# A one-core decoder step: TensorE's 32 experts written out, its next token count read in mid-block, one looped body on ScalarE and VectorE, the second biases in mid-way, the last keys' load one place earlier

## The chip, the cores and the metric

One core of one Trainium2 chip runs the whole program, all in 32-bit floats. The metric is the device time of one execution in microseconds (us), and the number to be compared is the median of the runs.

## The reference, cut to what matters

288 tokens (256 of a prompt, 8 x 4 new ones) go through one layer: a combined projection, dilated attention beside a state-space mixer, an output projection, and then a mixture of 32 experts of which each token takes four.

```python
logits = jnp.dot(h, w_router) + b_router
top_v, top_i = lax.top_k(logits, TOP_K)                    # 4 of 32
gates = jax.nn.softmax(top_v, axis=-1)
...
def expert_block(args):                                    # w1[e]: 1024 x 2048, w2[e]: 1024 x 1024
    a = jnp.dot(xb, w1[e]) + b1[e]
    x_glu = jnp.minimum(a[:, :D_FF], SWIGLU_LIMIT)
    x_lin = jnp.clip(a[:, D_FF:], -SWIGLU_LIMIT, SWIGLU_LIMIT)
    mid = x_glu * jax.nn.sigmoid(SWIGLU_ALPHA * x_glu) * (x_lin + 1.0)
    return jnp.dot(mid, w2[e]) + b2[e]
...
out = out.at[row_tok].add(ys * row_gate[:, None])          # back to the tokens, by gate
```

Every expert's weights are read whole: 12 MB each, 384 MB in all. Before that, eight batches of cached keys and eight of cached values are read (1.25 MB each).

## The kernel before, in words

**The front** is hand-ordered. SyncE (`sp`) issues all transfers of data in one queue, in program order. `load_keys(b)` brings the keys of batch b into one of two buffers and, from batch 2 on, first waits until TensorE has turned the 5 key tiles of each batch up to b-2 (`kt_ps`). `load_values(b)` brings values into one of four buffers. The last batches are issued in the order values 4, values 5, keys 7, values 6, values 7 (L435 to L439). TensorE turns the key tiles in `key_columns(n)` (L1414; batch 7 is n = 35 to 39), takes the scores in L1431 and L1433, and applies the values in `values(half)` (L1457). VectorE and ScalarE evict the key tiles in turn (L1016, L690).

**The expert stage.** The weights of an expert are 12 pieces of 1 MB, in the places of a ring of 21 slots, which lie in nine different tiles (`ring`, `kv_rows`, `tmp`, `w_glu`, `mixer`, `uni`, `accT`, `x`, `low`). So a slot's name repeats after 7 experts (`TURNS`), since 7 x 12 = 4 x 21. SyncE refills a slot (L491) as soon as TensorE has used its piece for the last time (`w_used`, and `out_ps` for the twelfth piece).

An expert's tokens are served in blocks of 32, so an expert with up to 32 tokens takes one block, one with up to 64 two, and so on; the weights are loaded once for all of them. `run_experts` finds the blocks of an expert with three nested loops over the count (L339 to L344), read from `cnt` (L337). In this input there are 51 blocks. The experts 0 and 1 come first, for their weights can be loaded before the routing is known; the others come in an order that spreads the full ones.

A block on TensorE (`pe_pass`): the first product, 8 pieces, four matmuls in quadrants each (L1739); adding the block before back to the tokens (L1716); gathering the tokens of the next block (L1684), for which it waits for `sel`, made by VectorE (L1248); transposes (L1764, L1769); the second product, 4 pieces (L1747); transposes of the gathered tokens (L1727) and the first bias of the next block (L1732). ScalarE's part is a sigmoid and two copies (L801 to L805). VectorE's (`next_block`) is the selection of the next block, the gating, four evictions, and eight small products for the gated selection (L1217, L1218). VectorE is thus one block ahead of TensorE in its loops, and reads two registers from memory for each expert (count and name), TensorE and ScalarE one.

On each of the three engines the expert loop is written as a loop of four passes over a body of 7 experts (L350), and four more experts behind it. TensorE adds the second biases for all tokens (`second_biases`, L1700) between the two, behind the 28th expert. SyncE has a loop of its own (L498), which is not changed.

Of the kernel before, what the change touches and what calls it, by code (L numbers as in the profile page):

```python
# [35 lines left out]
NTOK = SEQ + NS  # L36
# [21 lines left out]
NPIECE = 12  # L58
NSLOT = 21
TURNS = 7  # L60
WARM = 20


# [58 lines left out]
def decoder_step(nc, I, O):  # L122

    with ExitStack() as ctx:
# [189 lines left out]
        def landed(turn, k):  # L314
            return s_w[(NPIECE * turn + k) % NSLOT]
# [12 lines left out]
        def expert_at(eng, place):  # L328
            return eng.value_load(names_o[0:1, bass.ds(place, 1)], min_val=0, max_val=NEXP - 1)

        def run_experts(eng, block_of, named=False, between=None):

            done = eng.alloc_register()
            eng.reg_mov(done, 0)

            def expert(turn, e, before):
                count = eng.value_load(cnt[0:1, bass.ds(e, 1)], min_val=1, max_val=NTOK)  # L337
                name = expert_at(eng, e) if named else None
                with eng.Fori(0, 2 * CAP, CAP) as p:  # L339
                    with eng.If(count > p):  # L340
                        with eng.Fori(p, 2 * p + CAP, CAP) as o:
                            with eng.If(count > 2 * o - p):
                                with eng.Fori(2 * o - p, 6 * o - 4 * p + CAP, CAP) as c:
                                    with eng.If(count > c):  # L344
                                        n = eng.snap(done, min_val=0, max_val=NEXP * CHUNKS)
                                        first = nc.s_assert_within(c, 0, CHUNKS * CAP - CAP, skip_runtime_bounds_check_because="p, o, c of the three loops give 0; 1, 2; 3 to 8 times CAP")
                                        block_of(n, turn, name, before, first)
                                        eng.reg_add(done, done, 1)

            with nc.Fori(0, NEXP // TURNS, engines=[eng.engine], hint_back_edge=eng is nc.tensor) as g:  # L350
                for turn in range(TURNS):
                    expert(turn, g * TURNS + turn, g * (16 * TURNS * NPIECE // NSLOT))
            if between:
                between()
            for turn in range(NEXP % TURNS):
                expert(turn, NEXP // TURNS * TURNS + turn, 16 * (NEXP // TURNS * TURNS * NPIECE // NSLOT))
            return eng.snap(done, min_val=NEXP, max_val=NEXP * CHUNKS)


# [1 line left out]
        def _(sp):  # L361
# [56 lines left out]
            def load_values(b):  # L418
                load_cache("cache_v", v_cache[:, b % 4, :], b, S[f"vload{b % 4}"])
# [13 lines left out]
            sp.dma_start(w_out, I["w_out"][0].rearrange("(j p) n -> p j n", p=P)).then_inc(S["wout"], 16)  # L433
            sp.wait_ge(S["pv"], 1)
            load_values(4)  # L435
            load_values(5)
            load_keys(7)
            load_values(6)
            load_values(7)  # L439

# [178 lines left out]
        def _(act):  # L619
# [176 lines left out]
            act.wait_ge(S["gT_ps"], 1)  # L796
            A(gT[0:2 * NEXP, :], ps[0:2 * NEXP, 7, SEQ:SEQ + P], ACT.Copy)
            A(gT[2 * NEXP:, 0:NS], ps[2 * NEXP:3 * NEXP, 7, SEQ:SEQ + NS], ACT.Copy).then_inc(S["gT"], 1)
            def act_pass(n, turn, e, before, first):
                act.wait_ge(S["glin"], n + 1)  # L800
                A(sig, glu_b, ACT.Sigmoid, scale=ALPHA).then_inc(S["sgm"], 1)  # L801
                act.wait_ge(S["selT_ps"], n + 1)
                A(selT, ps[:, 5, 0:3 * P], ACT.Copy).then_inc(S["selT"], 1)  # L803
                act.wait_ge(S["out_ps"], n + 1)
                A(y, ps[:, 7, 0:NQ], ACT.Copy).then_inc(S["y"], 1)  # L805
# [16 lines left out]
        def _(dve):  # L822
# [432 lines left out]
                dve.wait_ge(S["sel"], n + 1)  # L1255
                gated_selection(bc(gate[:, bass.ds(e, 1), :].rearrange("p e t -> p (e t)").unsqueeze(2), [P, 3, CAP]))

            def dve_pass(n, turn, e, before, first):

                with dve.If(n > 0):  # L1260
                    next_block(n, e, first)
# [22 lines left out]
        def _(pe):  # L1284
# [446 lines left out]
                for q in range(4):  # L1731
                    mm(hidden(q), pick[quarter(q), :], b1_rows[quarter(q), :].rearrange("p (g n) -> p g n", g=2), start=True, stop=False, skip_group_check=True)  # L1732

            def pe_pass(n, turn, e, before, first):

                def first_product(k):
                    pe.wait_ge(landed(turn, k), before + loads(turn, k))
                    for q in range(4):
                        ins = mm(hidden(q), xe[:, k % 2, quarter(k // 2)], slot(turn, k)[:, :, NQ * q:NQ * q + NQ], start=False, stop=(k == 7),  # L1739
                                 skip_group_check=True)  # L1740
                    return ins

                def second_product(k):
                    pe.wait_ge(landed(turn, k), before + loads(turn, k))
                    for m in range(2):
                        for q in range(4):
                            ins = mm(ps[quarter(q), 7, 0:NQ], mt[:, m, quarter(k - 8)], slot(turn, k)[:, m, NQ * q:NQ * q + NQ],  # L1747
                                     start=(k == 8 and m == 0), stop=(k == 11 and m == 1), skip_group_check=True)
                    return ins

                pe.wait_ge(S["xe"], n + 1)
                for k in range(8):
                    ins = first_product(k)
                    if k == 7:
                        ins.then_inc(S["hid"], 1)
                    else:
                        ins.then_inc(S["w_used"], 1)
                pe.wait_ge(S["y"], n + 1)
                sum_back(0)
                sum_back(1).then_inc(S["w_used"], 1)  # L1760
# [62 lines left out]
```

## Time and profile before

| | |
|---|---|
| median of 3 runs | 1233.45 us (1232.19 to 1235.42) |
| the profiled execution | 1228.69 us, of which the profile's span is 1226.9 us |
| TensorE matmuls busy | 1087.5 us, 89% |
| VectorE, ScalarE busy | 412.0 us (34%), 218.4 us (18%) |
| queue of all data transfers | 445.00 MB, 89.8% of the 16 DMA engines' span |
| TensorE's mean granted clock | 0.949 |

The expert stage runs from 252 us to 1214 us of the span. The shares are means over the span; a stage can be bound by something that has a lower share in the whole. The profile says "issue" where an engine waited for nothing that it shows, which takes in the time of the engine's own register, branch and load-register instructions.

### The profile page before, as it was taken

What the parts mean: (1) busy time and instruction counts of PE and PEld (TensorE: products, weight loads), DVE (VectorE), ACT (ScalarE), POOL (GpSimd) and SP (SyncE); (2) the same over time, 40 slices, a digit from 0 to 9 for tenths busy, and PEclk for the clock granted to TensorE, in tenths of its full rate; (3) what the DMA queues carried; (4) which work ended last, traced back from release to release, by engine and by line L of the source; (5) the groups of instructions that cost most, each with busy time, mean ns of one, the idle gap of its engine ahead of it and who ended that gap; (6) DMA issues with size and microseconds to landing.
All of it is one profiled execution on the core that took longest, in us unless ns stands there. A gap on an engine that the chain in (4) does not pass through costs nothing.

```text
span 1226.9 us, 29914 instructions
## 1 busy us (share of the span) xinstructions
PE 1087.5 (89%) x10891; PEld 500.8 (41%) x10892; DVE 412.0 (34%) x1237; ACT 218.4 (18%) x402; POOL 81.8 (7%) x117
## 2 busy tenths in 40 slices
PE   8997889999988798999998786899989968999985
PEld 7775455444433333344433232244334422444442
DVE  4999665442212222222222221122222211222221
ACT  3214432311101011111111010011111100110111
POOL 2179300000000000000000000000000000000000
PEclk8998999999989998999999798799989998998999
DMA  8617775946999999998999999999999999999996
GB/s 231 231 44 237 267 272 218 357 193 272 419 420 419 421 413 419 420 417 333 419 421 419 419 419 419 421 384 420 419 418 376 418 420 421 412 419 419 419 420 248
DMA packets 81042, 446.46 MB, mean 364 GB/s; under 512 B 16801, under 2 KB 18145, under 8 KB 32033
## 3 DMA queue, kind: packets, MB, share of 16 engines
q1 hardware_dynamic: 80928, 445.00, 89.8%
q8 instruction: 65, 1.06, 0.4%
q14 instruction: 49, 0.39, 0.1%
HBM read 442.46 MB, written 2.51 MB: 363 GB/s over the span
## 4 chain that ended last, share of the span: by engine, by line
PE 62%; DMA 13%; SPq 12%; issue 7%; DVE 3%; ACT 1%; DVEq 1%; POOL 0%; POOLq 0%
PE ps L1739 21%; PE ps L1747 11%; SPq L491 10%; DMA ring<-in_w_moe_dram 6%; PE ps L1684 4%; PE ps L1332 4%; PE ps L1716 3%; PE ps L1732 3%; PE ps L1604 2%; DMA low<-in_w_moe_dram 2%; DMA uni<-in_w_moe_dram 2%; DMA kv_rows<-in_w_moe_dram 2%; PE ps L1714 1%; PE ps L1727 1%; PE ps L1764 1%
## 5 line engine op out<-in xcount | busy, mean ns | idle before, releaser
L1739 PE MATMUL ps<-ring,uni 128*32 128x512 f32 x2008 | 250.7, 638 | 50.8 <-issue 35.1
L1739 PEld LDWEIGHTS ps<-ring,uni 128*32 128x32 f32 x2008 | 64.4, 115 | 229.7 <-issue 193.4
L1233 DVE TENSOR_SCALAR uni<-ps 128x256 f32<-128x256 f32 x51 | 21.6, 424 | 298.2 <-PE ps L1739 298.2
L1747 PE MATMUL ps<-ring,uni 128*32 128x256 f32 x1696 | 100.3, 381 | 7.4 <-DMA ring<-in_w_moe_dram 7.4
L801 ACT ACTIVATE uni<-uni 128x256 f32<-128x256 f32 x51 | 21.2, 416 | 427.0 <-DVE uni L1233 427.0
L1254 DVE COPY uni<-ps 128x256 f32<-128x256 f32 x50 | 21.2, 425 | 211.2 <-PE ps L1727 211.2
L1684 PE MATMUL ps<-uni 128*32 128x256 f32 x1248 | 80.1, 390 | 8.3 <-DVE uni L1248 8.0
L801 ACT ACT_TABLE_LOAD x51 | 65.4, 1283 | 85.1 <-issue 85.1
L1747 PEld LDWEIGHTS ps<-ring,uni 128*32 128x32 f32 x1696 | 51.9, 110 | 46.5 <-DMA ring<-in_w_moe_dram 11.8
L1332 PE MATMUL ps<-accT,ring 128*128 128x288 f32 x256 | 66.4, 418 | 0.3 <-issue 0.3
L1716 PE MATMUL ps<-uni 32*128 32x256 f32 x832 | 62.1, 414 | 0.0
L1248 DVE TENSOR_TENSOR uni<-low,uni 128x96 f32 x50 | 12.9, 259 | 143.5 <-issue 133.6
L1716 PEld LDWEIGHTS ps<-uni 32*128 32x128 f32 x832 | 39.1, 192 | 47.5 <-issue 46.0
L1332 PEld LDWEIGHTS ps<-accT,ring 128*128 128x128 f32 x256 | 49.3, 195 | 15.4 <-issue 2.1
L1732 PE MATMUL ps<-uni 32*32 32x512 f32 x416 | 55.1, 600 | 0.0
L1684 PEld LDWEIGHTS ps<-uni 128*32 128x32 f32 x1248 | 35.8, 111 | 44.7 <-issue 18.1
L1739 PE MATMUL ps<-tmp,uni 128*32 128x512 f32 x320 | 42.3, 644 | 11.4 <-issue 6.3
L803 ACT ACTIVATE uni<-ps 128x384 f32<-128x384 f32 x51 | 25.0, 490 | 146.7 <-PE ps L1769 146.7
L805 ACT ACTIVATE uni<-ps 128x256 f32<-128x256 f32 x51 | 19.5, 383 | 174.8 <-PE ps L1747 174.8
L1217 DVE TENSOR_TENSOR uni<-uni 128x64 f32<-128x64 f32 x204 | 44.5, 218 | 1.4
L1242 DVE COPY uni<-ps 128x256 f32<-128x256 f32 x51 | 21.7, 425 | 65.6 <-PE ps L1764 65.6
L1218 DVE TENSOR_TENSOR uni<-uni 32x32 f32<-32x32 f32 x204 | 37.0, 182 | 2.5
(390 smaller groups left out, 1264.9 us busy)
## 6 DMA issues: line engine op xcount, KB each, us to landing
ring<-in_w_moe_dram SPq DMA_DIRECT2D x222, 1024.0 KB, 24.1
tmp<-in_w_moe_dram SPq DMA_DIRECT2D x36, 1024.0 KB, 24.4
kv_rows<-in_w_moe_dram SPq DMA_DIRECT2D x18, 1024.0 KB, 25.3
w_glu<-in_w_moe_dram SPq DMA_DIRECT2D x18, 1024.0 KB, 26.3
mixer<-in_w_moe_dram SPq DMA_DIRECT2D x18, 1024.0 KB, 25.7
uni<-in_w_moe_dram SPq DMA_DIRECT2D x18, 1024.0 KB, 26.1
accT<-in_w_moe_dram SPq DMA_DIRECT2D x18, 1024.0 KB, 26.1
x<-in_w_moe_dram SPq DMA_DIRECT2D x18, 1024.0 KB, 26.3
```

The costliest lines, as they stand in the source:

```text
L491: sp.dma_start(slot(turn, k), piece(following[later - 1], k2)).then_inc(landed(turn, k), 16)
L801: A(sig, glu_b, ACT.Sigmoid, scale=ALPHA).then_inc(S["sgm"], 1)
L803: A(selT, ps[:, 5, 0:3 * P], ACT.Copy).then_inc(S["selT"], 1)
L1217: tt(selg[:, 0:2, q, :], sel[:, 0:2, :], gb[:, 0:2, :], ALU.mult)
L1218: ins = tt(selg[rows, 2, q, :], sel[rows, 2, :], gb[rows, 2, :], ALU.mult)
L1332: ins = mm(ps[:, 4 + n % 2, 0:NTOK], w_in[:, c // 4, j, P * (c % 4):P * (c % 4) + P], accT[:, j, :], start=(j == 0), stop=(j == J - 1))
L1604: ins = mm(ps[:, 4 * t + 2 * a + c, :], src[:, kb, t0:t0 + P], w_out[:, 4 * a + kb, 512 * c:512 * c + 512], start=(kb == 0), stop=(kb == 3))
L1684: ins = mm(ps[quarter(q), 6, 0:NQ], sel[:, t, :], h[:, t, NQ * q:NQ * q + NQ], start=(t == 0), stop=(t == 2), skip_group_check=True)
L1716: ins = mm(ps[:, q, NQ * t:NQ * t + NQ], selT[quarter(q), P * t:P * t + P], y[quarter(q), :], start=False, stop=True, skip_group_check=True)
L1732: mm(hidden(q), pick[quarter(q), :], b1_rows[quarter(q), :].rearrange("p (g n) -> p g n", g=2), start=True, stop=False, skip_group_check=True)
L1739: ins = mm(hidden(q), xe[:, k % 2, quarter(k // 2)], slot(turn, k)[:, :, NQ * q:NQ * q + NQ], start=False, stop=(k == 7), skip_group_check ...
L1747: ins = mm(ps[quarter(q), 7, 0:NQ], mt[:, m, quarter(k - 8)], slot(turn, k)[:, m, NQ * q:NQ * q + NQ], start=(k == 8 and m == 0), stop=(k ...
```

## The change

1. TensorE's expert loop is written out: 32 bodies behind one another, with no loop over groups. The waits for pieces become constants.
2. TensorE's count for an expert is read from memory in the block before, behind the first product and ahead of the wait for `y`, into a register of its own; at the expert's start it is only copied.
3. ScalarE and VectorE run one body in a loop of 32 passes.
4. The second biases are added behind the 16th expert (turn 15) and not behind the 28th.
5. The load of the keys of batch 7 is issued ahead of that of the values of batch 5.

```diff
+BIAS_TURN = 15
...
+        following_count = nc.tensor.alloc_register()
...
-            def expert(turn, e, before):
-                count = eng.value_load(cnt[0:1, bass.ds(e, 1)], min_val=1, max_val=NTOK)
+            def expert(turn, e, count):
                 name = expert_at(eng, e) if named else None
...
-            with nc.Fori(0, NEXP // TURNS, engines=[eng.engine], hint_back_edge=eng is nc.tensor) as g:
-                for turn in range(TURNS):
-                    expert(turn, g * TURNS + turn, g * (16 * TURNS * NPIECE // NSLOT))
-            if between:
-                between()
-            for turn in range(NEXP % TURNS):
-                expert(turn, NEXP // TURNS * TURNS + turn, 16 * (NEXP // TURNS * TURNS * NPIECE // NSLOT))
+            if eng is nc.tensor:
+                eng.reg_load(following_count, cnt[0:1, 0:1])
+                for turn in range(NEXP):
+                    expert(turn, turn, eng.snap(following_count, min_val=1, max_val=NTOK))
+                    if turn == BIAS_TURN:
+                        between()
+            else:
+                with nc.Fori(0, NEXP, engines=[eng.engine]) as e:
+                    expert(None, e, eng.value_load(cnt[0:1, bass.ds(e, 1)], min_val=1, max_val=NTOK))
...
             load_values(4)
+            load_keys(7)
             load_values(5)
-            load_keys(7)
             load_values(6)
...
-                    pe.wait_ge(landed(turn, k), before + loads(turn, k))
+                    pe.wait_ge(landed(turn, k), loads(turn, k))
...
+                if turn + 1 < NEXP:
+                    pe.reg_load(following_count, cnt[0:1, turn + 1:turn + 2])
                 pe.wait_ge(S["y"], n + 1)
                 sum_back(0)
```

## Rows read from the trace of the kernel before

**Rows 1.** The page's 40 slices of the span: what the DMA engines moved.

```profile
GB/s 231 231 44 237 267 272 218 357 193 272 419 420 419 421 413 419 420 417 333 419 421 419 419 419 419 421 384 420 419 418 376 418 420 421 412 419 419 419 420 248
```

**Rows 2.** Waits of the DMA queue on SyncE: us in total, times, longest.

```profile
SPq L491 <- PE ps L1739: 212.1, 119, 28.3
```

**Rows 3.** Windows of 10 us: busy by engine, TensorE's clock, DMA share, GB/s.

```profile
550.00:560.00 10.00, 10.00 (x139) 5.01 (x135) 2.45 (x7) 0.91 (x2) 0.00 (x0) 1.00 0.82 340
560.00:570.00 10.00, 10.00 (x102) 3.32 (x98) 3.11 (x13) 2.08 (x3) 0.00 (x0) 1.00 0.58 227
800.00:810.00 10.00, 10.00 (x126) 3.89 (x122) 2.04 (x10) 2.05 (x3) 0.00 (x0) 1.00 0.78 310
```

**Rows 4.** TensorE's timeline, experts 0 and 17: start, us, line, count, idle before.

```profile
268.20 7.07 PE L1739 MATMUL ps<-ring,uni 128*32 128x512 f32 x64
...
283.92 7.07 PE L1739 MATMUL ps<-ring,uni 128*32 128x512 f32 x64
...
764.09 1.06 PE L1739 MATMUL ps<-uni 128*32 128x512 f32 x8 [1.40 <-DMA uni<-in_w_moe_dram]
```

**Rows 5.** Timeline of VectorE and TensorE at the first edge between groups.

```profile
462.07 0.26 DVE L1248 TENSOR_TENSOR uni<-low,uni 128x96 f32 x1 [10.97 <-issue]
...
462.38 2.00 PE L1684 MATMUL ps<-uni 128*32 128x256 f32 x24 [2.68 <-DVE uni L1248]
...
475.40 9.49 PE L1739 MATMUL ps<-ring,uni 128*32 128x512 f32 x64 [3.79 <-issue]
```

**Rows 6.** Line 350 there, by sequencer: ns min/median/max, first and last start.

```profile
L350 DVEq COMPARE_BRANCH  x1: 66/66/66, 451.4 to 451.4; - x1
L350 DVEq FUSED_REGOPS  x1: 74/74/74, 456.8 to 456.8; - x1
L350 PEldq COMPARE_BRANCH  x1: 2140/2140/2140, 471.0 to 471.0; - x1
...
L350 ACTq FUSED_REGOPS  x1: 71/71/71, 471.6 to 471.6; - x1
```

**Rows 7.** From expert 0 to 1 on TensorE: its timeline, and its load.

```profile
301.23 1.06 PE L1739 MATMUL ps<-mixer,uni 128*32 128x512 f32 x8 [1.51 <-issue]
...
L337 PEldq TENSOR_LOAD <-cnt x1: 316/316/316, 299.2 to 299.2; - x1
```

**Rows 8.** The front: SyncE, TensorE, the chain, and the page's small key loads.

```profile
159.50 0.42 SPq L408 DMA_DIRECT2D ring<-in_cache_k_dram  x1
...
157.37 1.09 PE L1414 MATMUL ps<-low,ring 128*128 128x128 f32 x8
...
168.29 0.66 PE L1414 MATMUL ps<-low,ring 128*128 128x128 f32 x4 [3.26 <-DMA ring<-in_cache_k_dram]
...
170.52 1.12 PE L1414 MATMUL ps<-low,ring 128*128 128x128 f32 x4
...
186.80 4.50 PE L1457 MATMUL ps<-ring,tmp 128*32 128x512 f32 x40
...
161.37 6.88 DMA ring<-in_cache_k_dram
...
ring<-in_cache_k_dram SPq DMA_DIRECT2D x32, 64.0 KB, 4.8
```

**Rows 9.** Two successive refills at that edge: issue, and time to landing.

```profile
L491 SPq DMA_DIRECT2D ring<-in_w_moe_dram x1: 333/333/333, 446.4 to 446.4; - x1
...
DMA to landing us min/median/max: 16.5/16.5/16.5
...
L491 SPq DMA_DIRECT2D ring<-in_w_moe_dram x1: 332/332/332, 447.2 to 447.2; - x1
...
DMA to landing us min/median/max: 19.2/19.2/19.2
```

**Rows 10.** TensorE's timeline: second biases, and expert 16's wait for pieces.

```profile
1115.43 5.88 PE L1700 MATMUL ps<-kv_rows,gT 32*128 32x256 f32 x24 [0.41 <-issue]
...
734.27 1.07 PE L1739 MATMUL ps<-ring,uni 128*32 128x512 f32 x8 [2.16 <-DMA ring<-in_w_moe_dram]
```

More of the change, by code:

```diff
@@ L346, in expert @@
                                         first = nc.s_assert_within(c, 0, CHUNKS * CAP - CAP, skip_runtime_bounds_check_because="p, o, c of the three loops give 0; 1, 2; 3 to 8 times CAP")
-                                        block_of(n, turn, name, before, first)
+                                        block_of(n, turn, name, first)
                                         eng.reg_add(done, done, 1)
-            with nc.Fori(0, NEXP // TURNS, engines=[eng.engine], hint_back_edge=eng is nc.tensor) as g:
-                for turn in range(TURNS):
-                    expert(turn, g * TURNS + turn, g * (16 * TURNS * NPIECE // NSLOT))
-            if between:
-                between()
-            for turn in range(NEXP % TURNS):
-                expert(turn, NEXP // TURNS * TURNS + turn, 16 * (NEXP // TURNS * TURNS * NPIECE // NSLOT))
+            if eng is nc.tensor:
[7 more added lines that the diff above has]
+                    expert(None, e, eng.value_load(cnt[0:1, bass.ds(e, 1)], min_val=1, max_val=NTOK))
             return eng.snap(done, min_val=NEXP, max_val=NEXP * CHUNKS)
@@ L798, in _, with act_pass @@
             A(gT[2 * NEXP:, 0:NS], ps[2 * NEXP:3 * NEXP, 7, SEQ:SEQ + NS], ACT.Copy).then_inc(S["gT"], 1)
-            def act_pass(n, turn, e, before, first):
+            def act_pass(n, turn, e, first):
                 act.wait_ge(S["glin"], n + 1)
@@ L1256, in next_block, with dve_pass @@
                 gated_selection(bc(gate[:, bass.ds(e, 1), :].rearrange("p e t -> p (e t)").unsqueeze(2), [P, 3, CAP]))
-            def dve_pass(n, turn, e, before, first):
+            def dve_pass(n, turn, e, first):
                 with dve.If(n > 0):
@@ L1732, in first_bias, with pe_pass @@
                     mm(hidden(q), pick[quarter(q), :], b1_rows[quarter(q), :].rearrange("p (g n) -> p g n", g=2), start=True, stop=False, skip_group_check=True)
-            def pe_pass(n, turn, e, before, first):
+            def pe_pass(n, turn, e, first):
                 def first_product(k):
-                    pe.wait_ge(landed(turn, k), before + loads(turn, k))
+                    pe.wait_ge(landed(turn, k), loads(turn, k))
                     for q in range(4):
@@ L1743, in second_product @@
                 def second_product(k):
-                    pe.wait_ge(landed(turn, k), before + loads(turn, k))
+                    pe.wait_ge(landed(turn, k), loads(turn, k))
                     for m in range(2):
```

## The prediction, as it was made before the changed kernel ran

> **What bounds the kernel now.** I read the page's slices first. From the eleventh on the DMA engines move 419 to 421 GB/s in most of them, with a few slices below [rows 1]. TensorE's matmuls look as busy (89% of the span), and the queue's waits name TensorE too: SyncE stood 212.1 us until it gave slots back [rows 2]. But a slot that comes back late costs nothing as long as other pieces are still queued; only where the rate falls was the queue empty. The expert stage is therefore bound by the stream of weights, and by TensorE in its holes alone. With 420 GB/s as full, the windows from 550 to 570 lack 10 x (1 - 340/420) + 10 x (1 - 227/420) = 6.5 us and that from 800 lacks 2.6 [rows 3]; the slice of 376 (920 to 951) lacks 30.7 x (1 - 376/420) = 3.2 [rows 1]; smaller dips add under 1.5. TensorE can give back some 13 us here in all, and what counts is why each hole is there.
>
> A hole needs an expert of three blocks: its slots come back only in the third, so nothing is refilled for two blocks, 15.72 us each (268.20 to 283.92 [rows 4]), while the ring has 21 - 12 = 9 slots for what is ahead. At expert 17 TensorE had caught up with the stream and waited for its pieces in the first block (764.09 [rows 4]); the hole of 2.6 us came all the same. It belongs to the ring's size, and no faster TensorE closes it. At expert 9 the hole was 6.5: about 4 us of it are TensorE's lateness.
>
> **Why it was late.** The edge between groups of 7, at 451 to 485. VectorE's branch at 451.4 is followed by its next instruction only at 456.8 [rows 6], and its selection starts 10.97 us after its last work; TensorE stood 2.68 us for it, and 3.79 us at its own edge [rows 5], with a branch of 2.14 us in it [rows 6]. The first product behind that took 9.49 us [rows 5] where 7.07 is the usual time [rows 4]: the clock had fallen. ScalarE's first instruction behind the same branch ran at 471.6, when TensorE's branch had begun 0.6 us before [rows 6]. Seven bodies of ScalarE's few instructions can be jumped over for nothing, seven of VectorE's can't.
>
> **Parts 1 and 3, the loops.** Removed between experts 5 and 9: the wait for VectorE, 2.7, and an estimated 1.5 behind it (the gather took 2.00 us in place of 1.5); at TensorE's edge 3.8 - 0.8 = 3.0; 2.4 of clock; and what part 2 gives in four transitions, about 3. That is some 13 us, where 4 were late. So TensorE now reaches expert 9 waiting for pieces, and the hole shrinks from 6.5 to the 2.6 of expert 17: **-4.0 us**. The third edge lies ahead of the hole of 920 to 940: 3.2 to 2.6, **-0.7**. The other holes stay. VectorE's new loop jumps back over one body, 32 times. Its loops over an expert's blocks jump back over nearly that body now, and from one block to the next of expert 0 TensorE runs with no idle time [rows 4], so I cost these jumps at nothing. What covers them is the first product: 7.07 us, against at most 10.97 - 5.4 = 5.6 until the selection without the fetch. If that cover goes, see the slower rival.
>
> The Trainium skill (Runtime: NRT & Kernel Launch, Instruction fetch mechanics) says that instructions are prefetched in sequence only, that a taken branch out of the pages held stalls for a fetch, and that kernels therefore prefer to be unrolled. For VectorE and ScalarE this speaks against the change, which has them jump 32 times and not 4. If one body fitted no window it would be the slower rival below. VectorE's 5.4 us against ScalarE's few tenths agree with the rule; that one body of VectorE's stays inside, the trace shows for the inner loops alone.
>
> **Part 2, the count.** From expert 0 to 1 TensorE stands 1.51 us, with a load of 0.32 us in it [rows 7]; with its address and the check behind it that is about 0.8 us, for one copy of 0.1. So -0.7 on each of 31 transitions, 22 us of TensorE's time, of which the holes above have already taken what counts. The load moved behind the first product runs while the last matmuls drain, and I cost it at nothing. Fully exposed it is 0.4 us a block, which counts in the two blocks without refills of the six three-block experts: at most +5.
>
> **Part 4, the biases.** They take 5.88 us at 1115 [rows 10], hidden by the stream. Behind expert 15, expert 16's first product waits for pieces (2.16 us for one [rows 10]). A piece of 1.049 MB comes every 1.049/0.42 = 2.50 us and is used in 7.07/8 = 0.88, so over its last six pieces TensorE has 9.7 us to spare, more than 5.88: **0**. Were TensorE late there, the hole at expert 17 would take them: +6.
>
> **Part 5, the keys.** TensorE stood 3.26 us for the keys of batch 7, until 168.29. They were issued from 159.50, behind values 5, the last of the five transfers at 161.37, which took 6.88 [rows 8]. Moved ahead, they wait for key tile 29, done at 157.37 + 1.09 = 158.46 [rows 8]. SyncE stands about 1.4 us at that wait, with values 5, 6 and 7 and the stores of keys and values behind it; together they go out by the same time as before, and the values are needed at 186.80 [rows 8]. The keys' last small transfer goes out at 158.5 + 1.9 = 160.4 and takes 4.8 us (the median [rows 8]), with 1.25 MB less ahead of it: landed at 165.2. TensorE was ready at 168.29 - 3.26 = 165.03. So -3.1, and behind the wait the clock had fallen (four transposes took 1.12 us, not 0.66 [rows 8]), an estimated 1.1 in all. **-4.2** (bounds: -2, if the transfer takes a microsecond longer and the clock falls still; -4.4). This is ahead of the stream: expert 0's three blocks hold it back until the third gives slots, so all later refills shift in full.
>
> **What the rate doesn't show.** At the first edge two pieces issued at 446.4 and 447.2 land 16.5 and 19.2 us later, 3.5 us apart [rows 9] and not 2.50, with the rate in its windows unbroken, and no later piece makes it up. If VectorE's code is fetched through the same engines there, that goes: two such steps of 1 us at each of three edges, 0 to -6. One row supports it, so I take **-2.5**.
>
> **Sum.** -4.0 - 0.7 - 4.2 - 2.5 = -11.4 us. The profiled execution took 1228.7 (1226.9 of span and 1.8 around it) and would take 1217.3. The runs' median lies 4.8 above it; the same sum on 1233.45 gives **1222 us**.
>
> **Rivals.**
> - *The full fetch step comes back and the holes shrink further*: -14 to -17, 1218. For it: those late pieces stand at the edges. Chance 0.18.
> - *Only the keys count*: -2 to -4.2, 1229 to 1231. So if TensorE, caught up, makes holes as deep as it did when late. Against it: the hole at 9 is 2.5 times that at 17. Chance 0.14.
> - *The change doesn't do what it says*: the keys' wait turns into another, and the stream sets the rest: 1233. Against it: the chain of waits runs through that very transfer [rows 8]. Chance 0.06.
> - *Slower: VectorE's back edge stalls for a fetch each time.* Then each transition costs TensorE the 4.2 us of the first edge, 0.8 of its own, and up to 2.4 of clock. It needs 51 x 15.7 = 801 us for its blocks and 31 x 5.0 = 155 to 31 x 7.4 = 229 more. From 248, with 14 behind and 6.6 to the median: 1225 to 1299, say 1260. It decides from (362 x 2.50 - 801)/31 = 3.4 us a transition on (362 pieces come after the hold at expert 0). Against it: the inner loops' jumps. Chance 0.04.
> - *The forecast*: 0.58.
>
> **Numbers.** The forecast's own range is 1219 to 1226; for 8 in 10, with the neighbours, 1216 to 1230. Within 0.3% (3.7 us, about what a measurement of this kernel can tell from no change) is 1229.8 to 1237.1. Faster: 0.58 + 0.18 + 0.06 of the keys' case = 0.82; same: 0.08 of it and 0.05 = 0.13; slower: 0.04 and 0.01 of the third case = 0.05.
>
> **What would show it.** Right: no wait of TensorE for the cached keys near 168 and the expert stage some 4 us earlier; no selection of VectorE's with an idle time over 6 us named "issue"; TensorE's transitions under 1 us; holes of 2 to 3 us at experts 9, 17 and 21. Wrong: TensorE waiting for VectorE's selection at many experts; TensorE standing between the first product and L1716; a hole at expert 17 above 3 us, which would be the biases.

## The result, and the profile after

| | before | after |
|---|---|---|
| median in the first comparison (4 runs each) | 1232.82 us | 1218.68 us (1217.71 to 1220.04) |
| ratio to before, 95% interval | | 0.9887 (0.9862 to 0.9912) |
| median in a second comparison | 1230.51 us | 1220.39 us (1218.96 to 1222.24) |
| ratio to before, 95% interval | | 0.9916 (0.9893 to 0.9938) |
| the profiled execution, its span | 1228.69, 1226.9 us | 1217.71, 1215.9 us |

The change makes the kernel 10 to 14 us faster, about 1%. The forecast was 1222 us, with 1216 to 1230 as its range, and for the profiled execution 1217.3 against the 1217.71 that it took. Parts of the sum are off in both directions all the same, and one term was booked twice, so that the match to 0.4 us is in part luck.

Line numbers are 4 to 6 higher in the changed kernel: the first product is L1743, the gather L1688, VectorE's selection L1252, the refill L495.

The page of the changed kernel, its 40 slices and its two instruction queues, answers to [rows 1]:

```profile
GB/s 221 244 45 234 259 290 243 360 172 274 419 420 420 421 415 420 419 420 402 419 420 420 420 420 419 421 389 419 421 420 411 419 420 420 393 419 420 420 419 248
q8 instruction: 60, 0.98, 0.3%
q14 instruction: 27, 0.22, 0.0%
```

The slices of 333 and 376 are gone, and there is a new one of 393 near the end. Queue 14 had 49 instruction packets before and has 27.

Windows of the changed kernel around its four holes, with the columns of [rows 3]:

```profile
540.00:580.00 40.00, 39.38 (x458) 17.14 (x451) 10.76 (x39) 5.56 (x9) 0.00 (x0) 1.00 0.98 406
780.00:820.00 40.00, 39.39 (x454) 16.83 (x450) 10.88 (x42) 6.67 (x10) 0.00 (x0) 1.00 0.96 398
900.00:950.00 50.00, 48.86 (x571) 21.16 (x567) 15.18 (x60) 7.74 (x13) 0.00 (x0) 1.00 1.00 415
1020.00:1060.00 40.00, 38.75 (x444) 16.22 (x448) 11.04 (x44) 6.81 (x10) 0.00 (x0) 1.00 0.97 399
```

With 420 GB/s as full, these stretches lack 40 x (1 - 406/420) = 1.3, 2.1, 0.6 and 2.0 us, 6.0 together. In the kernel before the same four lack 6.5, 2.5, 3.3 and 0.7 (352, 394, 392 and 413 GB/s), 13.0 together. This sum is called "the holes" below.

TensorE's timeline of the changed kernel: the last keys, the third block of expert 0, the transition to expert 1, and the first product at what was the first edge between groups; then VectorE's selection for the gather ahead of that product, which is the counterpart of the one in [rows 5]:

```profile
165.49 0.66 PE L1418 MATMUL ps<-low,ring 128*128 128x128 f32 x4 [0.42 <-DMA ring<-in_cache_k_dram]
...
281.36 7.07 PE L1743 MATMUL ps<-ring,uni 128*32 128x512 f32 x64
...
297.87 1.06 PE L1743 MATMUL ps<-mixer,uni 128*32 128x512 f32 x8 [0.71 <-issue]
...
464.30 7.08 PE L1743 MATMUL ps<-ring,uni 128*32 128x512 f32 x64 [0.60 <-issue]
```
```profile
451.74 0.26 DVE L1252 TENSOR_TENSOR uni<-low,uni 128x96 f32 x1 [3.57 <-issue]
```

Where [rows 8] had 3.26 us there are 0.42. Where [rows 7] had 1.51 there are 0.71. Where [rows 5] had 3.79 and a product of 9.49 us there are 0.60 and 7.08, and VectorE's selection comes 3.57 us after its last work in place of 10.97: 7.4 us less. The jump of [rows 6], 5.4 us in the kernel before, takes 0.3 here. The rest is a second stop of the kernel before, behind the jump:

```profile
L1260 DVEq COMPARE_BRANCH  x1: 52/52/52, 459.1 to 459.1; - x1
...
L1247 DVEq ALU_OP  x1: 40/40/40, 461.8 to 461.8; - x1
```

From that branch to VectorE's next instruction it is 2.7 us, and 0.2 in the changed kernel. The trace has instruction packets of queue 14 starting at 454.9 and at 459.9, one within each stop.

The selection runs 50 times, in a one-body loop of 32 passes, and the waits (us in total, times, longest) give the longest "issue" ahead of it, 5.4 us:

```profile
DVE uni L1252 <- issue: 135.6, 44, 5.4
```

TensorE's work right ahead of expert 0, on its timeline, and the windows with the clock:

```profile
243.20 1.97 PE L1688 MATMUL ps<-uni 128*32 128x256 f32 x24 [0.35 <-DVE uni L1179]
...
246.99 1.93 PE L1736 MATMUL ps<-uni 32*32 32x512 f32 x8
248.98 8.01 PE L1743 MATMUL ps<-ring,uni 128*32 128x512 f32 x64
```
```profile
244.00:248.00 4.00, 4.00 (x34) 1.91 (x23) 2.53 (x14) 0.46 (x2) 0.00 (x0) 0.51 1.02 422
248.00:252.00 4.00, 3.94 (x28) 0.95 (x24) 3.44 (x19) 1.28 (x1) 0.00 (x0) 0.64 1.01 422
```

In the kernel before, both windows have the full clock. Here the granted clock is 0.51 and 0.64, near the lower of its two levels (1.2 and 2.4 GHz) for most of 8 us, behind a stretch (240 to 244) in which TensorE's matmuls were busy for 2.85 of 4 us. Such a stretch does not explain the fall by itself: in the kernel before, TensorE was busy for 2.73 us of 248 to 252, and expert 0's first product behind it took 7.07 us all the same. So expert 0's first product starts 3.5 us sooner (248.98, not 252.47) but its third block only 2.6 us sooner (281.36, not 283.92 [rows 4]).

### The profile page after: what moved, and what is told of

The parts are those of the page before. It is cut to its first block, busy times and chain, and to the rows that moved or that the text cites. A ratio compares the mean times of both kernels' runs of the same rounds, so it can differ in the third digit from the quotient of the medians.

```text
span 1215.9 us, 29965 instructions
## 1 busy us (share of the span) xinstructions
PE 1086.7 (89%) x10891; PEld 501.5 (41%) x10891; DVE 412.4 (34%) x1237; ACT 218.4 (18%) x402; POOL 82.1 (7%) x117
## 4 chain that ended last, share of the span: by engine, by line
PE 50%; DMA 22%; SPq 15%; DVE 5%; issue 3%; ACT 1%; POOL 0%; DVEq 0%; POOLq 0%
PE ps L1743 19%; SPq L495 14%; DMA ring<-in_w_moe_dram 10%; PE ps L1751 8%; PE ps L1688 4%; PE ps L1736 3%; PE ps L1720 3%; PE ps L1608 2%; DMA tmp<-in_w_moe_dram 2%; DMA low<-in_w_moe_dram 2%; DMA uni<-in_w_moe_dram 2%; DMA w_glu<-in_w_moe_dram 2%; DMA kv_rows<-in_w_moe_dram 2%; PE ps L1731 1%; PE ps L1718 1%
## 5 line engine op out<-in xcount | busy, mean ns | idle before, releaser
L1743 PE MATMUL ps<-ring,uni 128*32 128x512 f32 x2008 | 247.9, 626 | 37.2 <-DMA ring<-in_w_moe_dram 23.5
L1743 PEld LDWEIGHTS ps<-ring,uni 128*32 128x32 f32 x2008 | 66.8, 113 | 211.4 <-issue 143.8
L1237 DVE TENSOR_SCALAR uni<-ps 128x256 f32<-128x256 f32 x51 | 21.6, 425 | 288.3 <-PE ps L1743 288.3
L1688 PE MATMUL ps<-uni 128*32 128x256 f32 x1248 | 80.8, 393 | 0.3 <-DVE uni L1179 0.3
L1252 DVE TENSOR_TENSOR uni<-low,uni 128x96 f32 x50 | 12.9, 259 | 137.2 <-issue 135.6
L1688 PEld LDWEIGHTS ps<-uni 128*32 128x32 f32 x1248 | 36.0, 112 | 37.8 <-issue 20.9
L1743 PE MATMUL ps<-tmp,uni 128*32 128x512 f32 x320 | 40.7, 618 | 9.6 <-DMA tmp<-in_w_moe_dram 6.2
```

Of the source, the lines that this page charges most:

```text
L1688: ins = mm(ps[quarter(q), 6, 0:NQ], sel[:, t, :], h[:, t, NQ * q:NQ * q + NQ], start=(t == 0), stop=(t == 2), skip_group_check=True)
```

## The experiments

Two readings separate what the runs mix. **The start** is where the third block of expert 0 begins: all before it is the front, where both kernels differ by the keys alone. **The rest** is the span less the start; the stream then runs to the end with few gaps. The start scatters by several us from run to run. The rest agrees within 0.4 us in the six profiles of kernels that hardly differ behind the start (after, after_again, keys_back, scalar_7, vector_2, vector_4); before and keys_alone, which are the same there, differ by 2.3 us.

| kernel | median, us | ratio to before (95%) | span | start | rest | holes |
|---|---|---|---|---|---|---|
| before | | | 1226.9 | 283.9 | 943.0 | 13.0 |
| keys_alone | 1228.83 | 0.9985 (0.9965 to 1.0006) | 1230.4 | 285.1 | 945.3 | 13.0 |
| bodies_alone | 1224.71 | 0.9940 (0.9916 to 0.9963) | 1223.4 | 287.2 | 936.2 | 7.2 |
| vector_7 | 1224.32 | 0.9943 (0.9921 to 0.9965) | 1224.4 | 285.4 | 939.0 | 9.6 |
| tensor_7 | 1219.92 | 0.9914 (0.9890 to 0.9937) | 1214.6 | 278.2 | 936.4 | 6.0 |
| count_at_start | 1219.32 | 0.9915 (0.9885 to 0.9946) | 1217.1 | 280.4 | 936.7 | 6.1 |
| keys_back | 1222.81 | 0.9930 (0.9906 to 0.9954) | 1223.0 | 288.3 | 934.7 | 6.4 |
| after | 1218.68 | 0.9887 (0.9862 to 0.9912) | 1215.9 | 281.4 | 934.5 | 6.0 |
| after_again | 1220.39 | 0.9916 (0.9893 to 0.9938) | 1219.8 | 285.0 | 934.8 | 6.3 |
| scalar_7 | 1217.82 | 0.9906 (0.9882 to 0.9930) | 1215.6 | 280.7 | 934.9 | 6.1 |
| vector_2 | 1219.45 | 0.9917 (0.9891 to 0.9944) | 1216.9 | 282.3 | 934.6 | 6.0 |
| vector_4 | 1219.71 | 0.9911 (0.9888 to 0.9934) | 1218.6 | 283.8 | 934.8 | 6.5 |
| ring_20 | 1228.79 | 0.9981 (0.9961 to 1.0002) | 1228.4 | 284.7 | 943.7 | 12.0 |
| one_first | 1206.96 | 0.9821 (0.9789 to 0.9853) | 1201.2 | | | 5.6 |

The row "after" is the first comparison above (before 1232.82 us). The other medians belong to three more, in which before took 1230.51 (keys_alone, vector_7, tensor_7, after_again), 1229.53 (bodies_alone, count_at_start, keys_back, one_first) and 1231.25 us (scalar_7, vector_2, vector_4, ring_20). The start and the rest are from one profile each.

**after_again**: the changed kernel once more.

> The changed kernel itself, for a comparison beside the others. Both theories: 11 to 14 us below the kernel before, about 1219.

It took 1220.39 us, 10.1 less than before, where 11 to 14 were expected. Its profile starts 3.6 us later than that of the first comparison, and its rest is the same within 0.3 us. So a difference in start between two single profiles says little. A difference in rest of 2 us counts among kernels like the changed one; against the kernel before it is within what two profiles differ by.

**keys_alone**: the kernel before with part 5 alone.

```diff
             load_values(4)
+            load_keys(7)
             load_values(5)
-            load_keys(7)
             load_values(6)
```

> The kernel before with part 5 alone. Theory (the keys' wait held everything behind it): TensorE's 3.26 us wait near 168 falls under 0.5, and since the stream is held by expert 0 behind it, 2.5 to 4 us come off in the end: about 1229 to 1230. Rival (the transfer was hidden by the stream anyway): 0, about 1233.

1.7 us faster in the medians, with an interval that reaches past no change. TensorE's timeline there, the keys and expert 0's first product:

```profile
164.66 0.66 PE L1414 MATMUL ps<-low,ring 128*128 128x128 f32 x4 [1.29 <-DMA ring<-in_cache_k_dram]
...
251.12 9.58 PE L1739 MATMUL ps<-ring,uni 128*32 128x512 f32 x64 [0.70 <-issue]
```

The wait is 1.29 us in place of 3.26, where under 0.5 was expected. But the granted clock was down ahead of expert 0 here too, and its first product took 9.58 us, not 7.07. A gain was made at the keys, and 2.5 us were given back there; the start of this one profile is 1.2 us later than that of the kernel before.

**keys_back**: the changed kernel with that load in its old place (the same edit, undone).

> The changed kernel with the load of the last keys behind values 5 again. Theory after the run of that part alone (it gave 1.8 us of the 4.2 forecast, the clock falling before expert 0 took the rest): 1 to 3 us above the changed kernel, ratio 0.991 to 0.993, TensorE waiting about 3 us for cached keys near 168. Rival (the part is worth its 4.2 us, the single run was an unlucky one): 0.993 to 0.995. Rival (worth nothing, since the clock takes it all): 0.9885 to 0.9915.

Three rows of TensorE's timeline, first of keys_back, then of the changed kernel:

```profile
154.80 0.49 PE L1418 MATMUL ps<-low,ring 128*128 128x128 f32 x3
...
168.74 0.66 PE L1418 MATMUL ps<-low,ring 128*128 128x128 f32 x4 [3.62 <-DMA ring<-in_cache_k_dram]
...
173.10 0.62 PE L1514 MATMUL ps<-uni,kv_rows 128*64 128x256 f32 x2 [0.26 <-DVE mixer L983]
```
```profile
154.75 0.49 PE L1418 MATMUL ps<-low,ring 128*128 128x128 f32 x3
...
168.72 0.62 PE L1514 MATMUL ps<-uni,kv_rows 128*64 128x256 f32 x2 [0.72 <-DVE mixer L983]
```

From the same work at 154.8 to the same work behind the keys it is 18.30 us in one and 13.97 in the other: part 5 is worth 4.3 us at its place, wait and clock together. Over all profiles the waits and the starts agree with that. With the old order TensorE waits 3.2 to 3.6 us for these keys (before, bodies_alone, keys_back) and with the new one between nothing and 1.8; the starts of the three have a mean of 286.5, those of the ten others in the table 282.7, 3.8 us less. In the median it is 3.5 us against count_at_start of the same comparison, which has all the rest of the change but part 2. The interval holds the theory's 1 to 3 us and the rival's 4.2 both. The rest stays at 934.7: the keys touch nothing behind the start. That the order of the keys alone decides the clock before expert 0 is refuted: it was 0.98 and 0.50 in those two windows here, with the old order, and 1.00 and 1.00 in tensor_7 with the new one.

**bodies_alone**: the kernel before with part 3 alone.

```diff
+            if eng is not nc.tensor:
+                with nc.Fori(0, NEXP, engines=[eng.engine]) as e:
+                    expert(None, e, 0)
+            else:
...
```

> The kernel before with only the loops of VectorE and ScalarE changed to one body for an expert; TensorE keeps its groups of seven, the count at an expert's start, the biases at turn 28 and the keys in their old place. Theory (VectorE's code fetch at the edges made TensorE late for expert 9 and held one of the sixteen DMA engines back): no selection of VectorE's stands over 6 us; queue 14's instruction packets fall from 49 to about 27 while queue 8's stay at 65; the pieces at the first edge come 2.5 us apart, not 3.5; the hole at expert 9 shrinks from 6.5 by 3 to 4: ratio to before 0.9965 to 0.9975. Rival A (the count read at each expert's start is what keeps TensorE late): the hole stays over 5 us, ratio 0.998 to 1.000. Rival B (VectorE alone is the whole gain of the change): 0.991 to 0.993.

The rest falls from 943.0 to 936.2 and the holes from 13.0 to 7.2, and the median is 4.8 us lower. That is more than the theory's 3 to 4 us at expert 9, and most of what the whole change does behind the start; the ratio, 0.9940, lies between those expected by the theory and by rival B. The windows of bodies_alone:

```profile
540.00:580.00 40.00, 38.64 (x465) 16.71 (x467) 11.33 (x46) 7.30 (x11) 0.00 (x0) 1.00 0.94 388
780.00:820.00 40.00, 36.47 (x444) 15.49 (x436) 10.78 (x43) 5.61 (x10) 0.00 (x0) 1.00 0.98 404
900.00:950.00 50.00, 48.49 (x575) 21.05 (x571) 14.26 (x54) 8.07 (x13) 0.00 (x0) 1.00 0.99 406
1020.00:1060.00 40.00, 38.46 (x477) 17.15 (x469) 11.05 (x41) 6.05 (x10) 0.00 (x0) 1.00 1.00 410
```

Expert 9's hole is 3.0, expert 17's 1.5 and expert 21's 1.7, though TensorE keeps its own edges. Its timeline at the first of them:

```profile
474.07 6.51 PE L1743 MATMUL ps<-ring,uni 128*32 128x512 f32 x32 [3.71 <-issue]
```

So TensorE still stands 3.71 us there; what went is the wait for VectorE. (The row shows the first half of that product; the whole took 9.94 us, so the clock still falls there.) Queue 14 has 27 instruction packets and queue 8 its 65, as the theory had it: the 22 packets that went brought VectorE's code. Queue 14 is not VectorE's alone, though (see ring_20). And the two refills that landed 3.5 us apart in [rows 9]? Their counterparts in vector_7 (below), where VectorE's edges are kept and TensorE's are not, and then in bodies_alone:

```profile
L501 SPq DMA_DIRECT2D ring<-in_w_moe_dram x1: 332/332/332, 447.7 to 447.7; - x1
...
DMA to landing us min/median/max: 16.6/16.6/16.6
...
L501 SPq DMA_DIRECT2D ring<-in_w_moe_dram x1: 332/332/332, 448.6 to 448.6; - x1
...
DMA to landing us min/median/max: 19.2/19.2/19.2
```
```profile
L495 SPq DMA_DIRECT2D ring<-in_w_moe_dram x1: 333/333/333, 449.4 to 449.4; - x1
...
DMA to landing us min/median/max: 16.2/16.2/16.2
...
L495 SPq DMA_DIRECT2D ring<-in_w_moe_dram x1: 333/333/333, 450.3 to 450.3; - x1
...
DMA to landing us min/median/max: 17.8/17.8/17.8
```

0.9 us apart at issue and 3.5 at landing in one, 0.9 and 2.5 in the other. This late piece goes with VectorE's edge and not with TensorE's. Other pieces are late in bodies_alone too: one lands 3.6 us after the one before it at 460.6, behind a packet of queue 8 at 458.2.

**vector_7**: the changed kernel with VectorE alone in groups of seven bodies again.

```diff
-                with nc.Fori(0, NEXP, engines=[eng.engine]) as e:
-                    expert(None, e, eng.value_load(...))
+                size = 7 if eng is nc.vector else 1
+                with nc.Fori(0, NEXP // size, engines=[eng.engine]) as g:
+                    for i in range(size):
+                        e = g * size + i
+                        expert(None, e, eng.value_load(...))
+                for i in range(NEXP % size):
+                    ...
```

> The changed kernel with VectorE alone back at four passes over seven bodies. Theory (VectorE's jump over seven bodies made TensorE late and cost fetches): its selection starts over 10 us after its last work at each edge, pieces land some 2 us late there, and the time rises by 3 to 7 us, to 1222 to 1226. Rival (TensorE's own loop and count were what counted): 0 to 1 us more, about 1219.

1224.32 us, 3.9 more than the changed kernel of the same comparison; the rest grows by 4.2 (934.8 to 939.0), as the theory had it. VectorE's timeline at the first edge:

```profile
463.46 0.26 DVE L1258 TENSOR_TENSOR uni<-low,uni 128x96 f32 x1 [11.01 <-issue]
```

The stand of 11 us is back, TensorE waits for it three times (11.4 us in all, 5.1 at most), queue 14 has 46 packets. The holes are 2.4, 4.4, 2.3 and 0.6: the largest is now at expert 17, behind the second edge.

**tensor_7**: the changed kernel with TensorE in groups of seven again, the count still read ahead, the second biases behind the 28th expert. (The table of counts has one word more here, so that the last expert too can read ahead.)

```diff
-                for turn in range(NEXP):
-                    expert(turn, turn, eng.snap(following_count, ...))
-                    if turn == BIAS_TURN:
-                        between()
+                with nc.Fori(0, NEXP // TURNS, engines=[eng.engine], hint_back_edge=True) as g:
+                    for turn in range(TURNS):
+                        expert(turn, g * TURNS + turn, eng.snap(following_count, ...), ...)
+                between()
+                ...
```

> The changed kernel with TensorE alone back at four passes over seven bodies and four behind them, the biases between, the count still read in the block before. Theory (VectorE's edges were the cost, TensorE's own 3 us and the clock fall behind it lie inside its reserve): within 1 us of the changed kernel, 1218 to 1220. Rival (TensorE's loop was what counted): 4 to 8 us more, 1223 to 1227.

0.5 us less than the changed kernel in the medians (after_again), 1.6 more in the rest. The four holes are 6.0 as there; the 1.6 us stand in a fifth, ahead of the first edge:

```profile
430.00:440.00 10.00, 10.00 (x108) 3.84 (x109) 2.73 (x11) 0.89 (x2) 0.00 (x0) 1.00 0.92 353
```

TensorE's edges and the old place of the biases together cost under 2 us once VectorE's edges are gone. No run has one of the two alone.

**count_at_start**: the changed kernel with part 2 undone.

```diff
-                    expert(turn, turn, eng.snap(following_count, min_val=1, max_val=NTOK))
+                    expert(turn, turn, eng.value_load(cnt[0:1, turn:turn + 1], min_val=1, max_val=NTOK))
...
-                if turn + 1 < NEXP:
-                    pe.reg_load(following_count, cnt[0:1, turn + 1:turn + 2])
```

> The changed kernel with each expert's token count read at the expert's start again. Theory (the transitions are hidden by the stream, holes apart): every transition grows by 0.8 us, the five holes together from 7.0 to 7.5 to 9, time within 2 us above the changed kernel's: ratio to before 0.990 to 0.993. Rival (what TensorE loses at 31 transitions adds up to the lateness that makes the holes): holes of 10 or more, 4 to 5 us above the changed kernel, ratio 0.994 to 0.996. No effect: 0.989 to 0.991.

Its transition from expert 0 to 1, on TensorE's timeline:

```profile
297.36 1.07 PE L1740 MATMUL ps<-mixer,uni 128*32 128x512 f32 x8 [1.16 <-issue]
```

1.16 us, against 0.71 with the count read ahead: part 2 gives 0.45 us a transition and not 0.8, some 14 us of TensorE's time over 31, of which 2 show in the rest (936.7) and none in the holes (6.1). The theory's "within 2 us" holds; the size of a transition was wrong.

**scalar_7**: as vector_7, but ScalarE (`nc.scalar`) in groups of seven.

> The changed kernel with ScalarE's loop over groups of seven experts' bodies, as before. Theory (seven bodies of ScalarE's few instructions are jumped over for nothing): no difference, within 1.5 us of the changed kernel, ratio to before 0.9885 to 0.9925, holes of 7. Rival (ScalarE's code too is fetched at the edge, through the same DMA engines, and a piece of the 3 to 7 us that VectorE's loop gives is ScalarE's): 0.993 to 0.995, and steps of 1 us between pieces at the edges.

No difference: 934.9, holes 6.1, and 29 packets in queue 14. ScalarE's half of part 3 is worth nothing, as the prediction read from [rows 6].

**vector_2** and **vector_4**: as vector_7, with `size = 2` and `size = 4`.

> The changed kernel with VectorE's loop over groups of two experts' bodies, jumped back 15 times. If two bodies can be jumped over for nothing: no selection with more than 6 us of issue before it, 27 instruction packets in queue 14, holes of 7 together, ratio to before 0.9885 to 0.9925. If they can't: some 15 selections stand about 11 us, queue 14's packets go to 70 or more, TensorE waits for VectorE 2 to 3 us at each and the holes grow to 10 or more: ratio 0.994 to 1.002.

> The same with groups of four bodies, jumped back 7 times. Theory: between one body, which costs nothing, and seven, which cost 5.4 us a jump, the cost comes as a step once the group is longer than what VectorE keeps: 7 selections of about 11 us and 4 to 6 us in all, ratio 0.993 to 0.997, as with seven bodies. Rival (the cost grows with the distance jumped): selections of 7 to 9 us, ratio 0.990 to 0.993.

Both are as fast as one body: rests of 934.6 and 934.8, with 27 and 28 packets in queue 14. For four bodies both the theory (stands of about 11 us) and its rival (7 to 9 us) were wrong. VectorE's loop line at the first jump of vector_4 (as in [rows 6]: ns, first and last start), and the page's line of queue 14:

```profile
L360 DVEq COMPARE_BRANCH  x1: 72/72/72, 360.8 to 360.8; - x1
L360 DVEq FUSED_REGOPS  x1: 74/74/74, 361.2 to 361.2; - x1
```
```profile
q14 instruction: 28, 0.23, 0.0%
```

From the branch to the next instruction it is 0.4 us, where [rows 6] had 5.4 (451.4 to 456.8). So the step lies between a jump over four of these bodies and one over seven. The Trainium skill (Runtime: NRT & Kernel Launch, Instruction fetch mechanics) says that a taken branch whose target is not among the pages held has to wait until that page has been fetched. The runs agree: a jump of VectorE's costs nothing or some 5 us, by the length of the loop's body and not by the number of passes, 4, 8, 16 or 32.

**ring_20**: the changed kernel with one slot less.

```diff
-NSLOT = 21
-TURNS = 7
+NSLOT = 20
+TURNS = 5
...
-            fill(20)
```

> The changed kernel with 20 slots for pieces in place of 21 (the queue's refills in groups of 5 experts, since 5 x 12 pieces are 3 x 20 slots). Theory of the prediction (the holes left belong to the ring's size: at a three-block expert the stream has 8 slots ahead, not 9, of 2.5 us each): the four holes, 7.0 us together in the changed kernel, become 15 to 17, and the pause at expert 0 grows by 2.5: 10 to 13 us above the changed kernel, ratio to before 0.998 to 1.001. Rival (the holes left are TensorE's lateness, which a slot doesn't change): holes of 7 to 9, the pause at expert 0 alone, 2 to 4 us, ratio 0.991 to 0.994.

Nearer to the theory: 1228.79 us. That is 9 to 11 more than scalar_7, vector_2 and vector_4 of the same comparison, which have the changed kernel's rest, and the rest is 8.9 to 9.2 longer; the ratio, 0.9981, is at the lower end of the theory's. Windows of ring_20:

```profile
420.00:450.00 30.00, 30.00 (x350) 12.81 (x350) 8.98 (x34) 5.14 (x8) 0.00 (x0) 1.00 0.93 385
540.00:580.00 40.00, 39.44 (x476) 16.87 (x468) 10.77 (x43) 6.82 (x11) 0.00 (x0) 1.00 0.95 389
780.00:820.00 40.00, 37.82 (x451) 16.33 (x449) 11.27 (x45) 6.02 (x10) 0.00 (x0) 1.00 0.93 382
900.00:950.00 50.00, 47.88 (x563) 20.67 (x563) 13.57 (x52) 7.72 (x12) 0.00 (x0) 1.00 0.97 398
1020.00:1060.00 40.00, 38.03 (x433) 15.98 (x433) 11.44 (x41) 5.69 (x10) 0.00 (x0) 0.97 0.95 391
```

The four holes are 3.0, 3.6, 2.6 and 2.8 (12.0, not 6.3 as in after_again), and a fifth of 2.5 stands at 420 to 450, where after_again has 415 GB/s and lacks 0.4. A slot is worth 0.9 to 2.1 us in each hole, not the 2.5 of a piece. It did not have to be that much: a hole only opens once what is ahead has landed, and how far ahead the stream is when it begins varies.

The edit changes one thing more: SyncE's refills, too, are written in groups of `TURNS` bodies, of five experts here and of seven in all other kernels. The changed kernel's loop line on SyncE at its first edge, and then the page's line of queue 14 in ring_20:

```profile
L502 SPq COMPARE_BRANCH  x1: 58/58/58, 472.8 to 472.8; - x1
L502 SPq FUSED_REGOPS  x1: 59/59/59, 478.0 to 478.0; - x1
```
```profile
q14 instruction: 11, 0.09, 0.0%
```

SyncE stands 5.2 us at a jump over seven of its bodies, as VectorE did, and 0.3 over five (415.1 to 415.4 in ring_20), and 16 of queue 14's 27 packets go with it. So queue 14 brings SyncE's code as well, and this edge is still in the changed kernel. What it costs was not tried by itself; in ring_20 its absence should, if anything, make the slot look cheaper than it is.

**one_first**: the changed kernel with expert 1 ahead of expert 0.

```diff
-    tie = np.where(e < FIXED, 1e5 * (FIXED - e), NEXP - 1 - e)
+    tie = np.where(e < FIXED, 1e5 * (e + 1), NEXP - 1 - e)
...
-                sp.dma_start(slots[n], piece(turn, k)).then_inc(landed(turn, k), 16)
+                sp.dma_start(slots[n], piece(FIXED - 1 - turn, k)).then_inc(landed(turn, k), 16)
```

and the first selection, its bias row and its gates on VectorE are taken from expert 1.

> The changed kernel with the two experts whose pieces are loaded before the routing is known in the other order: expert 1 first, then expert 0, whose tokens need three blocks. Theory (a three-block expert gives no slot back for two blocks, and expert 0, the first, holds the stream for some 24 us with all slots full; as the second it holds it while fewer pieces are outstanding, since expert 1's twelve slots have come back): the stream's pause of 24 us shrinks by 12 to 16 us and the later pieces all come that much sooner: ratio 0.977 to 0.981, about 1203 to 1207 us. Rival A (TensorE bounds the stage after all, so the pause only moves into later waits of the stream): 0.988 to 0.992, as the changed kernel. Rival B (half): the pause shrinks but TensorE, with less ahead of it, makes deeper holes at experts 9 and 17: 0.982 to 0.987.

1206.96 us, 12.4 less than count_at_start in the same comparison (about 2 of that is part 2, by the rest), and 22.6 less than before. The window from 250 to 300 of the changed kernel and of one_first:

```profile
250.00:300.00 50.00, 49.29 (x575) 20.96 (x570) 14.98 (x59) 7.72 (x12) 0.00 (x0) 0.99 0.44 181
```
```profile
250.00:300.00 50.00, 46.72 (x554) 20.55 (x547) 13.38 (x51) 7.72 (x12) 0.00 (x0) 1.00 0.71 288
```

107 GB/s more over 50 us are 5.35 MB, at 420 GB/s 12.7 us of the 14.7 between the spans. The 12.7 contain what came of a start of TensorE's stage that was 2.6 us sooner in this profile (246.38, not 248.98), so the order itself is worth some 10 to 12. The four holes behind it stay as they are (5.6), which speaks for the first theory's mechanism and against rival B's deeper holes; the size, a ratio of 0.9821, is just outside the theory's 0.977 to 0.981, at the edge of rival B's. The version is the fastest here; it rests on which of the two fixed experts has three blocks in this input, so it is no choice for every input.

## Why the prediction was right, and where not

- **The bound, right.** All of the change behind the start shows where the prediction looked: the rest fell by 8.5 us (943.0 to 934.5; the rest of the kernel before is known to some 2 us), the holes by 7.0 (13.0 to 6.0). TensorE's 14 us of shorter transitions, undone in count_at_start, gave 2.
- **"It belongs to the ring's size, and no faster TensorE closes it", half right.** ring_20 shows that each hole deepens with a slot less. But the hole of 900 to 950, for which the step let 2.6 us stand, went to 0.6 with the same ring, and one at 1020 to 1060 grew from 0.7 to 2.0. What a hole costs also depends on how far ahead the stream is when the three-block expert begins. Expert 17's hole of 2.6 was no measure for the others. SyncE's loop changed along with the slot in ring_20.
- **Parts 1 and 3, -4.7 forecast, -7.0 measured in the holes.** Expert 9: 6.5 to 1.3, forecast 2.6. Expert 17: 2.5 to 2.1. Expert 21: 3.3 to 0.6, where -0.7 was forecast and -2.7 came. The last one: +1.3, not forecast. The cause was right and is now narrower: VectorE's loop alone gives 6.8 us of the rest (bodies_alone) and takes 4.2 when put back alone (vector_7). The two differ by 2.6, hardly more than two profiles of the kernel before do (2.3); that TensorE's written-out experts also make up for part of VectorE's lateness is possible and not shown. What TensorE's loop adds once VectorE's edges are gone is 1.6 us with the biases' place (tensor_7), ScalarE's loop adds nothing (scalar_7). The prediction put 5.4 us of VectorE's 10.97 down to the fetch; it was 7.4, for it missed the second stop.
- **"What the rate doesn't show", -2.5, was booked twice.** The cause was right for the pieces at VectorE's edge (vector_7 against bodies_alone), but late pieces there are in the changed kernel too. In the landing times from 300 to 1200, 15 pieces of the kernel before land over 3.0 us after the piece before and within 4 us of the start of an instruction packet; in the changed kernel it is 16. VectorE's have gone, and those behind other packets of queues 8 and 14 are there as before or new. And the term was added to the holes, while it is no time beside them. A piece's landing is told in sixteen parts, and there are sixteen DMA engines; at that edge of the kernel before, the last part came 1.2 us behind the first at 448.9 and 3.9 at 466.4, while the rate stayed full. What lags so has only to be made good at the end, where the spread was 3.5 us before and 3.1 after. Of the rest's 8.5 us only 1.5 lie outside the four holes. That the lag is taken back in the holes is argued from this, not tried. This -2.5 and the holes' missing -2.3 cancelled.
- **Part 5, -4.2, right in its place** (4.3 by keys_back), wait and clock. "All later refills shift in full" held in the step from the keys to the start only where the clock stayed up: the profiled pair kept 2.6. The bound of -2 had been put down to a later transfer and a clock that falls at the keys; it fell before expert 0. That the pair kept less than the 3.8 us between the mean starts of the two orders is the chance of two single profiles. In the medians the part shows as 1.7 (keys_alone) and 3.5 us (keys_back).
- **Part 2, 0 beyond the holes**: 2 us by the rest, unclear by the medians. A transition got shorter by 0.8 (1.51 to 0.71), where 0.7 was forecast for part 2 alone: the count read ahead is 0.45, and the remainder comes with TensorE's loop written out. The load behind the first product costs nothing that the trace shows.
- **Part 4, 0, right as far as shown.** TensorE waits for a piece 13 us behind the end of the biases, so the stream covers them:

```profile
720.35 4.63 PE L1704 MATMUL ps<-kv_rows,gT 32*128 32x256 f32 x24
726.42 7.34 PE L1743 MATMUL ps<-ring,uni 128*32 128x512 f32 x40 [1.44 <-issue]
...
737.78 1.06 PE L1743 MATMUL ps<-tmp,uni 128*32 128x512 f32 x8 [1.43 <-DMA tmp<-in_w_moe_dram]
```

- **The sum.** In profiled executions -11.0 against -11.4: the start gave 2.6, the holes 7.0, and 1.4 lie between them. That the total was met so closely is luck: the keys gave 1.6 less in this pair than forecast, the holes 2.3 more, and a term of 2.5 was not there. The rival "VectorE's back edge stalls each time" is refuted by the 5.4 us at most; "only the keys count" by the rest of keys_alone (945.3); the full fetch step by its being no time beside the holes. "Holes that shrink further", a part of that same rival, did come (6.0, not 8.3).

## What to carry to other kernels

Where a stream feeds an engine, price a change by the windows in which the stream's rate falls, and take any lateness of a single transfer that leaves the rate whole as part of the next such window, not as a term of its own. When an engine stands with nothing to wait for at the back edge of a loop, cut the looped body on that engine before touching the others: here one engine's loop was between half (vector_7) and four fifths (bodies_alone) of the gain behind the start. Look at the loop of the engine that issues the transfers too: here SyncE's jump is as long. Compare single profiles from an event behind the noisy part (here the third block of the first expert), and take several to learn how well that agrees: within 0.4 us for six of these kernels, within 2.3 for two others. And before tuning transitions, ask whether an item that blocks the ring need come first.

## What the runs showed of the hardware that was not expected

- VectorE jumps back over four of these bodies for nothing. Over seven it stands 7.4 us longer at an edge, in two stops, with 19 to 22 instruction packets more in all and late pieces. One, 2 and 4 bodies give rests of 934.5 to 934.8, seven give 939.0. SyncE does the same: seven of its bodies cost 5.2 us a jump, five 0.3.
- Code packets share the way with the data. Behind such a packet the last part of a piece comes up to about 1 us later against the first (twice at a VectorE edge), while the rate of 417 to 420 GB/s doesn't show it. It shows in the times to landing only. All 16 pieces of the changed kernel that land over 3.0 us after the piece before do so within 4 us of a packet's start. That the packet holds back one of the sixteen DMA engines is the likely reading; the trace doesn't name the engine.
- TensorE's clock before expert 0 was at its upper level in some profiles and at its lower in others, with the same work ahead of it: expert 0's first product took from 7.07 to 9.58 us over the thirteen profiles in which expert 0 comes first. Together with the keys' wait (nothing to 1.8 us with the new order) and differences that arise ahead of the keys, it makes the start scatter between 278.2 and 285.4 us over the ten profiles with the new order. What decides it was not tried.
